# Second query pair's squares, sums and root cut into pieces inside a mixer's head, and the state-space decay weighting moved behind the next unit's softmax work

## The reference

```
ux = adaln(xs, norm1_w, sh1x, sc1x) @ w_in            # also uc for the context tokens
pool_x = pool_mixer(ux[..., :o_ssd], pool_w, pool_scale)
ssd_c, ssd_x = ssd_bidirectional(...)                  # Mamba-2 scan, both directions, chunks of 128
q = rmsnorm(u[..., :ATTN_DIM].reshape(B, L, 4, 128), q_norm_w)     # QK-norm: square, sum, root
qx, kx = apply_axial_rope(qx, rope), apply_axial_rope(kx, rope)
attn_x = latent_attention(qx, concat([kc, kx]), concat([vc, vx]))
mix_x = concat([pool_x, ssd_x, attn_x]) @ w_out
...
scores = einsum('bclhn,bcshn->bhcls', Cc, Bc) * Lmat   # Gram matrix times a decay matrix, per chunk
y_diag = einsum('bhcls,bcshp->bclhp', scores, x)
y_off  = einsum('bclhn,bchpn,bhcl->bclhp', Cc, prev_states, exp(a_cs))
```

## Time and profile before

| | |
|---|---|
| time, median of 3 runs | 1579.82 us (1579.38 to 1581.22) |
| profiled execution, own time | 1580.66 us |
| span of its trace | 1578.8 us |
| PE busy | 1523.1 us, 96% of the span |
| DVE, ACT, POOL busy | 868.0, 595.1, 138.9 us |
| chain that ended last | PE 84%, DVE 7%, ACT 4%, issue 2% |

### The profile page before, as it was taken

How to read it: one execution, slowest core, us unless ns; L and a number is a source line. 1 busy time by engine, 2 the same in 40 slices (tenths; PEclk the granted TensorE clock), 3 DMA queues, 4 the chain that set the end, 5 groups by cost and what they waited for, 6 DMA issues and landing times.

```text
span 1578.8 us, 22083 instructions
## 1 busy us (share of the span) xinstructions
PE 1523.1 (96%) x8944; PEld 1374.1 (87%) x8944; DVE 868.0 (55%) x1174; ACT 595.1 (38%) x900; POOL 138.9 (9%) x150
## 2 busy tenths in 40 slices
PE   6999988999999999999999999998999999999998
PEld 4899857899999999999999998995778788888887
DVE  4678887546755545555553467457656333333333
ACT  6634477535422112221122345346646321222222
POOL 0230421020000000000000024023110000000000
PEclk9999999999999999999999999998999999999999
DMA  9556221023443333333431133312022333333322
GB/s 366 169 174 190 68 77 41 19 63 113 141 133 113 127 132 109 134 127 113 133 112 52 51 80 88 79 57 67 15 67 81 94 99 99 91 88 102 93 77 83
DMA packets 208105, 162.49 MB, mean 103 GB/s; under 512 B 9268, under 2 KB 191004, under 8 KB 207900
## 3 DMA queue, kind: packets, MB, share of 16 engines
q1 hardware_dynamic: 206588, 156.63, 32.0%
q10 hardware_dynamic: 1440, 4.78, 0.8%
HBM read 156.76 MB, written 2.15 MB: 101 GB/s over the span
## 4 chain that ended last, share of the span: by engine, by line
PE 84%; DVE 7%; ACT 4%; issue 2%; DMA 1%; SPq 0%; POOL 0%; DVEq 0%; ACTq 0%; POOLq 0%
PE banks L1874 70%; PE banks L1992 4%; PE banks L2143 2%; PE banks L2021 1%; PE banks L2049 1%; DVE mod_sum L1320 1%; DVE w_lo L1295 1%; PE banks L2120 1%; DMA raw<-in_w_in_dram 1%; DVE nrm L1397 1%; PE banks L2176 1%; DVE h_lo L1391 1%; DVE neg_max L1675 1%; PE banks L1826 1%; ACT nrm L932 1%
## 5 line engine op out<-in xcount | busy, mean ns | idle before, releaser
L1295 DVE TENSOR_TENSOR w_lo<-raw,w_hi 128x1056 fp32r<-128x1056 f32 x184 | 245.1, 1332 | 298.3 <-ACT w_hi L879 297.5
L1874 PE MATMUL banks<-h_hi,w_hi 128*128 128x384 f32 (+3 forms) x1296 | 387.2, 357 | 10.2 <-DVE h_lo L1391 4.7
L1874 PE MATMUL banks<-h_lo,w_hi 128*128 128x384 f32 (+3 forms) x1296 | 382.9, 354 | 0.0
L1874 PE MATMUL banks<-h_hi,w_lo 128*128 128x384 f32 (+3 forms) x1296 | 382.6, 353 | 0.0
L879 ACT ACTIVATE w_hi<-raw 128x1056 fp32r<-128x1056 f32 x184 | 198.3, 1078 | 245.1 <-PE banks L1874 227.4
L1874 PEld LDWEIGHTS banks<-h_hi,w_hi 128*128 128x128 f32 x1296 | 235.6, 189 | 40.2 <-DVE h_lo L1391 10.6
L1874 PEld LDWEIGHTS banks<-h_hi,w_lo 128*128 128x128 f32 x1296 | 238.0, 189 | 16.8
L1874 PEld LDWEIGHTS banks<-h_lo,w_hi 128*128 128x128 f32 x1296 | 237.7, 189 | 15.8
L1874 PE MATMUL banks<-g_hi,w_hi 128*128 128x384 f32 (+1 forms) x528 | 159.9, 357 | 0.0
L1874 PE MATMUL banks<-g_hi,w_lo 128*128 128x384 f32 (+1 forms) x528 | 159.3, 356 | 0.0
L1874 PE MATMUL banks<-g_lo,w_hi 128*128 128x384 f32 (+1 forms) x528 | 159.2, 355 | 0.0
(11 more groups left out here) (223 smaller groups left out, 1891.6 us busy)
## 6 DMA issues: line engine op xcount, KB each, us to landing
raw<-in_w_dram SPq DMA_DIRECT2D x120, 512.0 KB, 3.9
mod_ring<-in_w_mod_dram SPq DMA_DIRECT2D x96, 512.0 KB, 4.9
raw<-in_w_in_dram SPq DMA_DIRECT2D x32, 512.0 KB, 4.9
raw<-in_w_out_dram SPq DMA_DIRECT2D x16, 512.0 KB, 4.2
raw<-in_w_dram SPq DMA_DIRECT2D x16, 384.0 KB, 3.3
cb_rows<-cs_rows_dram SPq DMA_DIRECT2D x20, 256.0 KB, 3.4
x_in<-in_x_dram ACTq DMA_DIRECT2D x4, 512.0 KB, 8.2
out_dram<-x_out SPq DMA_DIRECT2D x8, 256.0 KB, 2.3
```

Source lines behind the costliest of these rows:

```text
L1295: dve.tensor_tensor(w_lo[n % 2][:, :], raw[n % 4][:, :], as_f32(w_hi[n % 2][:, :]), ALU.subtract).then_inc(lo_ready, 1)
L1874: ins = pe.matmul(to(p, a, b), ws[:, w], xs(k, a, b), start=(first and q == 0), stop=(last and q == 2))
```

## The change

Three things change in the list, and the list alone decides them:

- The squares of the second query pair (ACT) and their sums (DVE) are cut into two pieces each (`sq23`, `ss23`) and set between the head's other events; their root (ACT) moves from unit 0 into the head. The number of signals of these two steps goes from 3 to 4 a layer. In layer 1 the rotary of the first pair (`q01`, 3) also moves ahead of the k transposes and of state step 2.
- `ssd_w` moves from the start of a chunk's second unit to its end, behind the unit's S, exp, trP, PV and behind what `in_unit` hangs on it. `ssd_y` moves from the end of that unit to the start of the next.
- `("tr", "q", h)` moves from the end of a unit to a place ahead of `ssd`, or, in a chunk's second unit, between `ssd_w` and `ssd_y`.

```
-                ev += [("mod_total",), blocks[3], states[0], ("mod_turn",), blocks[4], states[1], ("q01", 2), states[2], ("q01", 3), blocks[5],
-                       ("tr", "k", 0), states[3], ("tr", "k", 1), ("tr", "q", 0), ("q23_squares",), states[4]]
+                ev += [("mod_total",), blocks[3], states[0], ("mod_turn",), ("sq23", 0, 0, 4), blocks[4], states[1], ("q01", 2), ("ss23", 0, 0, 4),
+                       states[2], ("q01", 3), blocks[5], ("tr", "k", 0), ("sq23", 1, 4, 6), states[3], ("ss23", 1, 4, 6), ("tr", "k", 1), ("tr", "q", 0),
+                       ("q23", 0), states[4]]
             else:
-                ev += [states[0], blocks[3], states[1], ("q01", 2), ("tr", "k", 0), states[2], ("q01", 3), ("tr", "k", 1), states[3],
-                       ("tr", "q", 0), ("q23_squares",), states[4]]
+                ev += [states[0], blocks[3], ("sq23", 0, 2, 4), ("sq23", 1, 4, 6), states[1], ("q01", 2), ("q01", 3), ("tr", "k", 0), ("ss23", 0, 2, 4),
+                       ("ss23", 1, 4, 6), states[2], ("tr", "k", 1), ("q23", 0), states[3], ("tr", "q", 0), states[4]]
...
             for u in range(len(units) + 3):
-                if last_c is not None:
-                    ev.append(("ssd_w", last_c, u))
+                if last_c is not None and u % 2:
+                    ev.append(("ssd_y", last_c))
+                    last_c = None
...
                 ev += in_unit.get(u, [])
                 gate_now = not todo and last_c is None
                 if last_c is not None:
-                    ev.append(("ssd_y", last_c))
-                    last_c = None
+                    ev.append(("ssd_w", last_c, u))
                 if gate_now and gates and gates[0][0] in ("gs", "gi"):
                     ev.append(gates.pop(0))
+                if u < len(units) and units[u][1] == (2 if l and units[u][0] == 1 else 1) and units[u][0] + 1 < ATT_HEADS:
+                    ev.append(("tr", "q", units[u][0] + 1))
                 if todo and u % 2:
...
+                    elif e[0] == "sq23":
+                        a, b = e[2:]
+                        act.wait_ge(tok_free, tok_count(l, 3) + b - tok_from(l, 3))
+                        act.activation(qk_sq_last[:, 2 * a:2 * b, :].rearrange("p a n -> p (a n)"),
+                                       qk[:, 1, a:b, :].rearrange("p t n -> p (t n)"), ACT.Square).then_inc(qksq_ready, 1)
...
+                    elif e[0] == "ss23":
+                        a, b = e[2:]
+                        dve.wait_ge(qksq_ready, l * INCS["qksq_ready"] + 3 + e[1])
+                        dve.tensor_reduce(qk_ss[:, 2, 2 * a:2 * b], qk_sq_last[:, 2 * a:2 * b, :], AX_X, ALU.add).then_inc(qkss_ready, 1)
```

More of the change, by code:

```diff
@@ L76 @@
     sq_ready=KC, acc_ready=KC - 2, acc_last=1, ss_ready=1, root_ready=1, rstd_ready=1, rstd_pe=1, rstd_out=1, t_ready=KC, h_hi_ready=KC,
-    h_lo_ready=KC, xp_hi_ready=KC, xp_lo_ready=KC, xp_used=KC - 1, xbc_ready=5, pads_zero=10, count_used=2, pooled_ready=2, qksq_ready=3, qkss_ready=3,
+    h_lo_ready=KC, xp_hi_ready=KC, xp_lo_ready=KC, xp_used=KC - 1, xbc_ready=5, pads_zero=10, count_used=2, pooled_ready=2, qksq_ready=4, qkss_ready=4,
     qkrt_ready=3, qkn_ready=3, rope_s_ready=6, qk_ready=3, dt_in=1, dt_exp=2, a_ready=1, cs_pe=1, cs_ready=3,
@@ L485, in mixer_events @@
             if l < DEPTH - 1:
-                ev += [("mod_total",), blocks[3], states[0], ("mod_turn",), blocks[4], states[1], ("q01", 2), states[2], ("q01", 3), blocks[5],
-                       ("tr", "k", 0), states[3], ("tr", "k", 1), ("tr", "q", 0), ("q23_squares",), states[4]]
-            else:
-                ev += [states[0], blocks[3], states[1], ("q01", 2), ("tr", "k", 0), states[2], ("q01", 3), ("tr", "k", 1), states[3],
-                       ("tr", "q", 0), ("q23_squares",), states[4]]
+                ev += [("mod_total",), blocks[3], states[0], ("mod_turn",), ("sq23", 0, 0, 4), blocks[4], states[1], ("q01", 2), ("ss23", 0, 0, 4),
+                       states[2], ("q01", 3), blocks[5], ("tr", "k", 0), ("sq23", 1, 4, 6), states[3], ("ss23", 1, 4, 6), ("tr", "k", 1), ("tr", "q", 0),
+                       ("q23", 0), states[4]]
+            else:
+                ev += [states[0], blocks[3], ("sq23", 0, 2, 4), ("sq23", 1, 4, 6), states[1], ("q01", 2), ("q01", 3), ("tr", "k", 0), ("ss23", 0, 2, 4),
+                       ("ss23", 1, 4, 6), states[2], ("tr", "k", 1), ("q23", 0), states[3], ("tr", "q", 0), states[4]]
             states = []
-            in_unit = {0: [("q23", 0), ("pool", 0), ("pool", 1)], 2: [("q23", 1)], 3: [("q23", 2)], 4: [("q23", 3)], 5: [("q23", 4)], 6: [("q23", 5)]}
+            in_unit = {0: [("pool", 0), ("pool", 1)], 2: [("q23", 1)], 3: [("q23", 2)], 4: [("q23", 3)], 5: [("q23", 4)], 6: [("q23", 5)]}
             if l == DEPTH - 1:
@@ L534, in mixer_events @@
                     ev.append(early.pop(0))
-                if u < len(units) and units[u][1] == (2 if l and units[u][0] == 1 else 1) and units[u][0] + 1 < ATT_HEADS:
-                    ev.append(("tr", "q", units[u][0] + 1))
             assert not todo and last_c is None and not states and not gates and not early
@@ L1024, in head_root @@
                     h0 = 2 * tok_from(l, 2) if seq else 0
-                    act.wait_ge(qkss_ready, l * INCS["qkss_ready"] + seq + 1)
+                    act.wait_ge(qkss_ready, l * INCS["qkss_ready"] + (seq + 1 if seq < 2 else 4))
                     act.activation(qk_rt[:, seq, h0:12], qk_ss[:, seq, h0:12], ACT.Sqrt, bias=eps[:, 0:1],
@@ L1096, in _ @@
                         act.activation(qk[:, 1, t, :], banks[:, i % 2, 0:256], ACT.Copy).then_inc(tok_free, 1)
-                    elif e[0] == "q23_squares":
-                        square_heads(2)
+                    elif e[0] == "sq23":
[3 more added lines that the diff above has]
+                                       qk[:, 1, a:b, :].rearrange("p t n -> p (t n)"), ACT.Square).then_inc(qksq_ready, 1)
                     elif e[0] == "w_out_tile":
@@ L1608, in _ @@
                     elif e[0] == "q23" and e[1] != 3:
-                        if e[1] == 0:
-                            reduce_heads(2)
-                        elif e[1] < 3:
+                        if 0 < e[1] < 3:
                             scale_heads(2, e[1] - 1)
@@ L1614, in _ @@
                             turned = rotate_first(2)
-                        else:
+                        elif e[1] == 5:
                             rotate_second(2, turned)
+                    elif e[0] == "ss23":
+                        a, b = e[2:]
+                        dve.wait_ge(qksq_ready, l * INCS["qksq_ready"] + 3 + e[1])
+                        dve.tensor_reduce(qk_ss[:, 2, 2 * a:2 * b], qk_sq_last[:, 2 * a:2 * b, :], AX_X, ALU.add).then_inc(qkss_ready, 1)
                     elif e[0] == "mod_steps":
```

## The result

The changed kernel takes 1597.78 us (median of 5 runs, 1596.92 to 1598.95) against 1580.98 us for the kernel before (5 runs, 1579.38 to 1582.98). The ratio is 1.0107, with a 95% interval of 1.0095 to 1.0119: slower by 16.9 us. The forecast was +6.5 us, with a range that ended at 1590.5. The sign was right and the size was not.

A forecast was written before the change was run, and what follows sets the result against it. PE was taken to bound the kernel, waiting in a ring over four engines. Layer 0 +1.9, layer 1 +4.1 and DVE with POOL +0.5 gave +6.5 us: median 1586.3 us, range 1581.0 to 1590.5.

The forecast's parts named there:

- measure of a chunk: In each chunk, an odd unit's maximum follows its w by at least 4.03 us; before, the distance was 4.68 to 5.35.
- The signs: Trace marks expected: exp of u1 at 204.5, one table load, shifted maxima, DVE and PE idle in u8, no "issue" waits.
- M7: Maximum of unit 7 in layer 0, expected level with 235.45 us, its time in the trace before.
- Head of layer 0: Earlier exp of u1 brings the maximum of unit 3 forward: -1.6 us, bounds -1.0 to -2.3.
- Head of layer 1: Exp of u1 about 1 us sooner, rotary earlier, PE's 3.86 us wait replaced: -0.5 us, between +1.0 and -2.5.
- u8 and the tile: In u8 the output-projection tile's remainder `w_lo` stands before w: +1.8 us in layer 0, +3.0 in layer 1.
- `w_hi` step: In layer 0's u8, ACT reaches `w_hi` 1.0 us sooner, bounds 0 and 2.25; w then starts at 245.9.
- DVE and POOL: Later w falls together with POOL's `e_cum` products in u4, u10 and layer 1's u6: 0 to 1.9 us, taken as 0.5.
- the clock falls too: Rival, chance 0.23: PE's clock falls in u8 while waiting for w, 1.9 us each; one place 1588.2 us, both 1590.1.
- Faster, by ACT's order: Rival, chance 0.10: earlier query copy removes both "issue" waits and `w_lo` hides under PE's PV: -3.8 us, 1576.0.
- Little left of it: Rival, chance 0.15: u8 costs its lower bounds, 0.5 and 2.0, layer 1's head gives 2.0: about +2 us, 1581.8.

The follow-up runs named there:

- warm_pe: The changed kernel with filler products on PE ahead of y, 3 in a chunk and 9 in u8's: 1594.04 us, ratio 1.0089 to the kernel before.
- head_only: The changed head, with the chunks and query transposes in the order of the kernel before: 1576.01 us, ratio 0.9968 to that kernel.
- head_and_query: Head and query transposes as in the change, w and y placed as in the kernel before: 1576.91 us, ratio 0.9975 to that kernel.
- the control: The kernel before with POOL's work shortened, part of the computation left out: 1577.33 us, ratio 0.9986; the changed kernel shortened likewise took 1589.61 us.

## Why the prediction was wrong

The step that failed is the **measure of a chunk**: "in the changed list a maximum follows its w by at least 1.29 + 2.74 = 4.03 us". The number is right as a floor (4.27 and 4.17 us in the u8 of `warm_pe`, with w alone and the clock full). The prediction then used the floor as the value, with POOL at 0.5 us in all and the clock left to a rival, and so credited each chunk with 0.65 to 1.32 us of shortening; in the changed kernel the distances were 4.66 to 6.70 us and not 4.03. When w starts was forecast well. The forecasts in the table's second column are what the prediction's terms make of the trace before: for u4 of layer 0, 220.79 - 215.85 plus 1.36 is 6.30 us.

| chunk | previous odd maximum to w: forecast, measured | w to next odd maximum: forecast, measured | w pair, us |
|---|---|---|---|
| layer 0, u4 | 6.30, 6.14 | 4.03, 6.02 | 1.95 |
| layer 0, u6 | 6.89, 7.03 | 4.03, 6.34 | 1.81 |
| layer 0, u8 | 10.45, 10.41 | 4.03, 6.48 | 1.29 |
| layer 0, u10 | 4.81, 4.76 | 4.03, 4.66 | 1.28 |
| layer 1, u4 | 6.51, 6.16 | 4.03, 6.70 | 2.35 |
| layer 1, u6 | 5.86, 5.71 | 4.03, 5.22 | 2.24 |
| layer 1, u8 | 9.29, 9.17 | 4.03, 5.41 | 1.29 |

The forecast in the third column is too small by 12.6 us in these seven rows and by 1.4 us in layer 0's u2. That is the miss: the terms of the changed trace add up to 19.1 us where I had 6.5; what stands ahead of w and the heads took 1.4 us off. (The first mixer of the changed trace starts 1.3 us earlier, so the span grew by less, 17.6 us to 1596.4.) Of these 14.0 us, 3.8 are w pairs stretched by POOL, and 7.7 are by the comparison with `warm_pe` the clock. Some 2.5 us are left that no run here takes apart, 0.8 of them in layer 0's u2, where PE was at half clock with the fillers too.

**The signs.** The ones of the mechanism came as predicted: one table load between the query copy and exp of u1, DVE idle for 3.0 us ahead of `w_lo` in u8 of both layers, PE idle for 5.60 and 4.41 us ahead of y there. The "issue" waits of layer 0's u8 and layer 1's u2 went, but a new one of 3.13 us stands ahead of the query transposes in layer 0's u2. The first sign that failed clearly was M7: it was to be level with 235.45 and came 5.1 us later (239.22, and 1.3 for the earlier start). M7 to M9 grew by 4.2 us in layer 0 and 3.7 us in layer 1, against forecasts of 1.8 and 3.0.

**Head of layer 0**, -1.6: right by itself (-1.9 in `head_only`). Exp of u1 is at 203.07 in the changed trace, 204.4 on the clock of the trace before; the forecast was 204.5. But M3 moved by -0.85 only, because w of u2 met POOL and PE was at half clock behind it. **Head of layer 1**, -0.5: too small for the head alone, which gave -2.6 there, beyond my bound of -2.5; with the chunks in their new order it was -0.1. The trace of the change hid this, and only `head_only` showed that the head is worth 5 us where the chunks keep their order.

**u8 and the tile.** The `w_hi` step held: its start moved up by 0.9 us against M7 (forecast 1.0), and w started where it was forecast. Its price was taken too low because PE's wait was priced only as long as it lasted (5.60 us); PE then ran y and the scores at half clock, 2.2 us more in layer 0 and 1.2 us in layer 1.

**DVE and POOL**, 0.5: mis-sized. w pairs alone grew by 4.8 us, and the comparison with the control gives 4.4 us, with the clock in it. I had counted three places by where w fell in the old trace, u10 among them, where the pair took 1.28 us. With w later it meets POOL in six, each of the two w products can be held once (in layer 0's u4 the second takes 1.21 us instead of 0.68), and in layer 1's u2 POOL is at its rotary, which I hadn't considered: one w product takes 1.74 us there. By the Trainium skill's rule (SBUF — State Buffer, section Who interferes with whom) the term in my prediction would have been 1.9. The trace agrees: a pair at 1.8 to 1.95 us is two w products of 0.64 us with 0.5 to 0.7 us of waiting, and a POOL product that nothing holds lasts 0.72 us. My 0.5 against it had no row behind it, and even 1.9 was too small, because the places were six.

**The rival "the clock falls too"** came true in both u8, at the cost that it named for layer 0 (1.9 us; measured 2.2). It also happened in u2, u4 and u6 of layer 0 and in u4 of layer 1, which neither the forecast nor the rival had. That a wait of 2.87 us had left the clock alone was no protection: in u6 a wait of 2.79 us stood ahead of a fall, after two chunks in which the clock had fallen already; what in the stretch ahead decides it was not taken apart here. The Trainium skill (TensorE: Matmul & The Clock Gate, Part 1) makes activity alone the condition; the trace agrees, since the time at half clock went from 34 us to 6.8 us when PE was given products without use. **"Faster, by ACT's order"** fell with `head_and_query`: the "issue" waits are no gain to be had by themselves. **"Little left of it"** had u8 at 0.5 and 2.0 us; it cost 4.2 and 3.7.

## What to carry to other kernels

A distance measured at its shortest is a floor; before it goes into a sum as a value, ask for each stretch what else will be running there, above all GpSimd beside a DVE product, and whether PE comes to it from a wait. When work is deferred on one engine, look at what already stands at the new place, and at who waits there: here the consumer's later place was free and the producer's later place cost 20 us. Where a change has two halves, time them apart: a head that gains 5 us by itself was hidden in a loss of 17, and beside the late w it gained next to nothing.

## What the hardware showed unexpectedly

PE's clock halved after waits of a length that had been harmless before (2.79 us in the changed u6, against 2.87 and 2.91 us with no fall before), and each such fall lengthened the way from w to the next odd maximum by 1.2 to 2.2 us, from 4.2 to 5.3 us at full clock. Filler products on an idle PE took the time at half clock from 34 to 6.8 us but were not free: 1.1 and 1.3 us in two chunks. Two DVE products that take 1.28 us alone, with both inputs in SBUF, took 2.35 us beside GpSimd, 1.8 times as long.
